# First turns of the experts: a routing cast by ScalarE, the shared down product split, y's last store on ScalarE's queue, another order of VectorE's work

## The reference, cut to what matters

```python
scores = sigmoid(tok @ router_w)
_, top_e = top_k(masked(scores + router_bias), 8)        # 4 of 8 groups, then 8 experts
wts = scores[top_e] / sum(scores[top_e]) * 2.5
for each block b of 128 tokens that chose expert e:
    xb = x_pad[rows[b]]
    hb = silu(xb @ w_gate[e]) * (xb @ w_up[e])
    y[rows[b]] += (hb @ w_down[e]) * wts
y = y + (silu(tok @ s_gate) * (tok @ s_up)) @ s_down
```

## Time and profile before

| | |
|---|---|
| median of three executions | 2744.7 us |
| the profiled execution | 2747.92 us, its span 2746.1 us |
| TensorE matmul busy | 2630.2 us, 96% |
| VectorE busy | 2019.8 us, 74% |
| ScalarE busy | 1367.0 us, 50% |
| granted TensorE clock, mean | 0.983 |

### The profile page before, as it was taken

How to read it: one execution, slowest core, us unless ns; L and a number is a source line. 1 busy time by engine, 2 the same in 40 slices (tenths; PEclk the granted TensorE clock), 3 DMA queues, 4 the chain that set the end, 5 groups by cost and what they waited for, 6 DMA issues and landing times. The chain is left out here.

```text
span 2746.1 us, 42114 instructions
## 1 busy us (share of the span) xinstructions
PE 2630.2 (96%) x13712; PEld 1193.1 (43%) x13715; DVE 2019.8 (74%) x5289; ACT 1367.0 (50%) x3178; POOL 603.2 (22%) x458
## 2 busy tenths in 40 slices
PE   7999999999899999999999799998999999999995
PEld 2444666545433443434434375453333334333332
DVE  4996566585588888888877555755897888888865
ACT  1113666343166666666656241332665666666651
POOL 0000000111023332332323211100232332333322
PEclk9999999999999999999999999998999999999998
DMA  9777400201399999999989732016999999999996
GB/s 374 252 266 200 183 17 17 78 36 47 147 366 362 335 331 342 359 347 357 371 302 366 223 115 91 31 46 250 339 338 345 311 377 346 352 372 299 327 343 203
DMA packets 151301, 697.56 MB, mean 254 GB/s; under 512 B 25189, under 2 KB 30565, under 8 KB 98857
## 3 DMA queue, kind: packets, MB, share of 16 engines
q1 hardware_dynamic: 104252, 556.14, 51.9%
q0 software_dynamic: 46528, 136.62, 20.1%
q10 hardware_dynamic: 304, 2.11, 0.2%
HBM read 597.50 MB, written 128.47 MB: 264 GB/s over the span
## 5 line engine op out<-in xcount | busy, mean ns | idle before, releaser
L1812 ACT ACTIVATE xT<-xt_blocks 32x256 f32<-32x256 f32 x2208 | 913.5, 414 | 38.4 <-DVE xt_blocks L1638 10.8
L1889 PE MATMUL exG<-ring,xT 128*32 128x512 f32 (+2 forms) x2352 | 684.8, 601 | 0.9 <-DMA ring<-in_exp_w_up_dram 0.6
L1653 DVE STREAM_TRANSPOSE ex_hT<-ex_h 32x64 f32<-32x64 f32 x2240 | 528.6, 236 | 33.6
L1889 PEld LDWEIGHTS exG<-ring,xT 128*32 128x32 f32 (+2 forms) x2352 | 240.3, 141 | 342.3 <-issue 338.5
L1550 POOL DMA_INDIRECT wide_t<-u_scratch,idx x144 | 152.8, 1061 | 946.2 <-DVE idx_out L1687 773.7
L1563 POOL DMA_INDIRECT y_scratch<-wide_w,idx_out x192 | 322.3, 1679 | 146.5 <-issue 80.1
L1922 PE MATMUL exD<-ring,ex_hT 128*32 128x512 f32 (+2 forms) x1176 | 351.6, 599 | 2.4 <-DVE wide_w L1679 2.4
L1889 PE MATMUL exG<-wide_w,xT 128*32 128x512 f32 (+2 forms) x1072 | 325.0, 601 | 11.1 <-issue 11.1
L1889 PE MATMUL exG<-wide_t,xT 128*32 128x512 f32 (+2 forms) x1024 | 315.3, 599 | 3.3 <-DVE xT L1632 2.1
L1824 ACT ACTIVATE ex_e<-exG 128x256 f32<-128x256 f32 x142 | 54.4, 383 | 524.7 <-PE exG L1889 524.7
L1643 DVE TENSOR_TENSOR ex_h<-ex_e,exG 128x256 f32<-128x256 f32 x142 | 86.5, 609 | 179.0 <-ACT ex_e L1824 178.6
(11 more groups left out here) (366 smaller groups left out, 3277.7 us busy)
## 6 DMA issues: line engine op xcount, KB each, us to landing
ring<-in_exp_w_gate_dram SPq DMA_DIRECT2D x64, 1024.0 KB
ring<-in_exp_w_up_dram SPq DMA_DIRECT2D x64, 1024.0 KB
ring<-in_exp_w_down_dram SPq DMA_DIRECT2D x64, 1024.0 KB, 12.1
wide_t<-in_exp_w_gate_dram SPq DMA_DIRECT2D x34, 1024.0 KB
wide_t<-in_exp_w_up_dram SPq DMA_DIRECT2D x34, 1024.0 KB
wide_t<-in_exp_w_down_dram SPq DMA_DIRECT2D x34, 1024.0 KB
wide_w<-in_exp_w_gate_dram SPq DMA_DIRECT2D x32, 1024.0 KB, 10.9
wide_w<-in_exp_w_up_dram SPq DMA_DIRECT2D x32, 1024.0 KB, 17.2
```

Of the source, the lines that this page charges most:

```text
L1653: last = dve.transpose(hT[m * UNIT:(m + 1) * UNIT, par].rearrange("p (k t) -> p k t", k=FK)[:, :, a * UNIT:(a + 1) * UNIT], hid[a * UNIT:( ...
L1812: last = act.activation(xT[m * UNIT:(m + 1) * UNIT, par, :, a * UNIT:(a + 1) * UNIT], parts[a * UNIT:(a + 1) * UNIT, m], ACT.Copy)
L1889: last = pe.matmul(psG[par][p:p + m], xT[:, par, k, p:p + m], ring[s % RING][:, 0:2, k * FF:(k + 1) * FF], start=k == 0, stop=k == KT - 1)
```

## The change

In **mix**: the first cast of the weights goes from VectorE (L1222) to ScalarE, which waits for VectorE's copy of the places first; the subtraction that uses it is moved ahead of the wait for turn 0's row numbers. TensorE does the first half of `down(7)` ahead of turn 0's row numbers and the second half behind them. y's last store is issued by ScalarE behind its own copy instead of by SyncE.

In **experts**: VectorE's first turns are written in another order, and TensorE's `index(2)`, `index(3)` are put between steps of `gate_up(0)`, `index(4)` between steps 2 and 3 of `gate_up(1)`; `turn_rows(1)` follows `gate_up(0)` directly.

```diff
@@ mix, SyncE
-                            sp.wait_ge(yo_done, t + 1)
-                            sp.dma_start(y_dram[layer]...[t * P:(t + 1) * P, 0], yo[t % 2]).then_inc(yo_out[t % 2], 16)
+                            else:
+                                sp.wait_ge(yo_done, t + 1)
+                                keep_y(sp, t)
@@ mix, VectorE
                         link(dve.tensor_copy(place[:], psM[:, :, 0:E]))
+                        dve.sem_inc(place_done, 1)
...
-                        dve.tensor_copy(moving[:, :, :, 3], psM[:, :, E:])
+                        dve.wait_ge(high_done, 1)
+                        link(tt(rest, psM[:, :, E:], moving[:, :, :, 3], ALU.subtract))
                         link0 = Links(dve, idx_own)
                         dve.wait_ge(first_mm, 1)
...
-                        link(tt(rest, psM[:, :, E:], moving[:, :, :, 3], ALU.subtract))
@@ mix, ScalarE
                         turn_h(a + 3)
+                        act.wait_ge(place_done, 1)
+                        act.activation(moving[:, :, :, 3], psM[:, :, E:], ACT.Copy).then_inc(high_done, 1)
                         store(7)
+                        act.wait_ge(yo_done, NT)
+                        keep_y(act, NT - 1)
@@ mix, TensorE
                         last.then_inc(ranked_mm, 1)
+                        down(7, (0,))
...
                         last.then_inc(first_mm, 1)
-                        down(7)
+                        down(7, (1,))
@@ experts, VectorE
                         indices(0, 0, 2)
-                        onehot(2, 0)
                         indices(1, 1, 2)
                         rows(0, 0, 2)
+                        onehot(2, 0)
+                        onehot(3, 1)
                         indices(2, 0, 2)
-
-                        onehot(3, 1)
+                        onehot(4, 0)
+
                         rows(1, 1, 2)
                         indices(3, 1, 2)
-                        onehot(4, 0)
                         turn_blocks(2, 0)
                         indices(4, 0, 2)
@@ experts, TensorE
                         turn_rows(0, 0, 16)
+                        gate_up(0, 0, range(0, 3))
                         index(2, 0)
-
-                        gate_up(0, 0)
+                        gate_up(0, 0, range(3, 6))
+                        index(3, 1)
+                        gate_up(0, 0, range(6, KT))
                         turn_rows(1, 1, 16)
-                        index(3, 1)
+                        gate_up(1, 1, range(0, 3))
                         index(4, 0)
+                        gate_up(1, 1, range(3, KT))
                         for b in range(1, T):
                             par = b % 2
-                            gate_up(b, par)
+                            if b > 1:
+                                gate_up(b, par)
```

More of the change, by code:

```diff
@@ L1051, in mix @@
                     "r_exp", "r_mask_done", "r_cnt_mm", "r_pos_mm", "r_iota"))
+                place_done, high_done = sem("r_place_done"), sem("r_high_done")
                 rank_done, key_mm, ids_done, cat_done, turn_mm, catT_done, ranked_mm = (sem(n) for n in (
@@ L1054, in mix, with keep_y @@
                 GONE = -3.0e38
+                def keep_y(eng, t):
+                    eng.dma_start(y_dram[layer].rearrange("(r j) d -> r j d", j=2)[t * P:(t + 1) * P, 0], yo[t % 2]).then_inc(yo_out[t % 2], 16)
                 with nc.Block(no_gpsimd_drain=True) as block:
@@ L1078, in _ @@
                                 load_down(sp, ex, 0)
-                            sp.wait_ge(yo_done, t + 1)
-                            sp.dma_start(y_dram[layer].rearrange("(r j) d -> r j d", j=2)[t * P:(t + 1) * P, 0], yo[t % 2]).then_inc(yo_out[t % 2], 16)
+                            else:
+                                sp.wait_ge(yo_done, t + 1)
+                                keep_y(sp, t)
                     @block.gpsimd
@@ L1342, in score, with down @@
                             last.then_inc(l_mm, 1)
-                        def down(t):
+                        def down(t, some=(0, 1)):
                             if t == 0:
                                 pe.wait_ge(wd_done, 1)
-                            pe.wait_ge(hT_done, t + 1)
-                            after(pe, yo_done, t, 1)
-                            for c in range(2):
+                            if some[0] == 0:
+                                pe.wait_ge(hT_done, t + 1)
+                                after(pe, yo_done, t, 1)
+                            for c in some:
                                 for k in range(FK):
@@ L1352, in down @@
                                                      start=k == 0, stop=k == FK - 1)
-                            last.then_inc(d_mm, 1)
+                            if some[-1] == 1:
+                                last.then_inc(d_mm, 1)
                         for t in range(NT):
@@ L1879, in turn_rows, with gate_up @@
                             last.then_inc(X_mm, 1)
[L1881 to L1887, removed]
+                        def gate_up(b, par, some=range(KT)):
+                            if some[0] == 0:
+                                for s, _, _, _, _ in turns[b]:
+                                    if first[s] == b:
+                                        pe.wait_ge(w_in[s % RING], 32 * (s // RING + 1))
+                                columns_ready(pe, b)
+                                after(pe, h_done, b, 2)
+                            for k in some:
                                 for s, _, p, m in pieces(turns[b]):
@@ L1890, in gate_up @@
                                                      start=k == 0, stop=k == KT - 1)
-                            last.then_inc(g_mm, 1)
+                            if some[-1] == KT - 1:
+                                last.then_inc(g_mm, 1)
                         def gate_up_over(b, i):
```

## The result

| | median | runs | ratio to before, 95% interval |
|---|---|---|---|
| before, beside the changed kernel | 2746.18 us | 8 | |
| changed kernel | 2755.14 us | 8 | 1.0031 [1.0020, 1.0041] |

The change makes the kernel slower: 0.0031 of 2746 us is 8.5 us (5.5 to 11.3). The forecast was +3.4 us, 2748.1 us, with a range of 2739.0 to 2752.5; 2755.14 lies above it.

What follows compares the result with a forecast made beforehand. TensorE, busy 96%, was taken as the bound, with early expert turns held by weight loads and VectorE's list. Terms -0.3 (layer 0), +2.5 (layer 1), +1.2 (clock) gave +3.4 us, 2748.1 us, range 2739.0 to 2752.5.

Steps and rivals of the forecast that it cites:

- Half of `down(7)` fits the idle: End of mix: half of down(7), 1.84 us, fits TensorE's 2.13 us idle; y is issued 1.65 us earlier in layer 0.
- w3 is no longer last: Layer 0: w3 up lands at 771.3, ahead of gate_up(2) at 772.3, so the load no longer holds it.
- forecast 2.5: Layer 1 experts: index(4) inside gate_up(1) makes index(5) start at 1922.65 instead of 1920.17, a loss of 2.5 us.
- the prediction's stall of layer 0: Layer 0 experts: TensorE ends gate_up(1) at 765.2 and waits 3.0 us for index(5), released by VectorE's onehot(5).
- the term -0.3 of the sum: Layer 0 experts: gate_up(2) starts at 772.3 against 772.60, so 0.3 us of the 1.9 gained is kept.
- The term of 0.6 us a layer: Stall ahead of index(5), both layers: a clock fall costing 1.6 us, 4 chances in 10, 1.2 us in all.
- The fall of before at 761.0: Layer 0: the existing 3.2 us low-clock stretch; gate_up(1) was forecast without it, ending at 765.2.
- The cast: Mix: moved from VectorE, where it took 1.87 us, to idle ScalarE; price taken as 0.7 us, bounded by 1.87.
- The next block: After mix, layer 0: begins near 739.4 instead of 741.15, worth 1.8 us to its first instructions.
- y's landing: y's last store lands 1.2 us earlier in both layers; bounds 0 to 1.65 us in layer 0, 0 to 3.3 in layer 1.
- The slower one: Rival, chance 0.15: index(4) behind the weights' wait bounds both layers and lowers the clock; +7.0 us, 2751.7 us.
- The faster rival: Rival, chance 0.18: gate_up(1)'s earlier start is kept in layer 0, layer 1 gains y's 3.3 us; -6.5 us, 2738.2 us.

Runs made afterwards that it cites:

- e3: Changed kernel with index(2) ahead of gate_up(0) and onehot(2) ahead of indices(1), as before the change; ratio to before 1.0017.
- e7: Kernel before with one edit alone, index(2) moved behind the first three steps of gate_up(0); ratio to before 1.0020.
- e4: Changed kernel with index(4) ahead of gate_up(1) instead of behind its third step; ratio to before 1.0032.
- e6: Changed kernel with TensorE's stall ahead of index(5) filled by unread transposes, 44 in layer 0 and 16 in layer 1; ratio to before 1.0020.
- e8: Changed kernel with index(2) ahead of gate_up(0), index(4) ahead of gate_up(1), onehot(5) ahead of hidden(0) and spread(0); ratio to before 0.9999.
- e10: e8 plus unread transposes in two TensorE waits, 14 ahead of down(0) in layer 0, 22 ahead of gate_up(1) in layer 1; ratio to before 0.9978.
- e1: Kernel before with only the mix edits, the experts' order left as it was; ratio to before 0.9998.

## Why the prediction was wrong

**Right.** The direction, up, was forecast. TensorE is busy for the same time. Half of `down(7)` fits the idle. `gate_up(1)` of layer 0 starts at 757.80, as forecast, and `index(4)` at 760.45 (forecast end 760.8). Part of that is luck: `gate_up(0)` started at 746.55 and not 745.8, and was shorter than forecast by as much. w3 is no longer last in layer 0: its down load is issued at 748.04 and lands 24.8 us later, 772.8, against 774.97. Layer 1 has the stall of 2.67 us where about 3 was forecast, behind `index(4)`; `gate_up(2)` is 1.8 us later, forecast 2.5. No clock fall there. e3's 2.77 us is the prediction's stall of layer 0, with `index(2)` out of the way.

**The step that failed.** "TensorE ends gate_up(1) ... and waits 3.0 us for index(5) ... Layer 0 gains 0.3 us of the 1.9." The wait was 6.12 us, and layer 0 lost 5.5: the term -0.3 of the sum should have been +5.5. The prediction charged `index(2)` its 0.36 us on TensorE and took VectorE's list to be free at `indices(4)`. It followed the dependents of `index(4)` and not those of `index(2)`: row numbers, a gather by GpSimd of 9 to 11 us from issue to landing, and `turn_blocks(2)`, which stands ahead of `indices(4)` in VectorE's list. Before, `index(2)`'s gather went out at 747.92 and VectorE reached `turn_blocks(2)` at 759.34; with a landing 11.1 us behind the issue it had 0.3 us of slack. The change moved its issue by 5.3 us. e7 shows that this alone brings such a delay, e4 that `index(4)`, which the prediction followed, was not last in layer 0.

**The clock.** The term of 0.6 us a layer (a fall of 1.6 us with 4 chances in 10) stood for a stall of 3 us. In layer 0 the fall came and cost 2.7 us in `down(0)`, shown by e6; in layer 1 none came. Behind a stall as long as the forecast one it cost 1.7 us in e3 and 2.9 in e7 (5.40 and 6.56 less 3.70). The fall of before at 761.0 did go, as the forecast's end of `gate_up(1)` at 765.2 had it; the wait behind took the gain.

**Sizes that were off without changing the sign.** The cast: 0.7 taken, 1.89 measured, as long as VectorE's own 1.87, just past the bound given, and VectorE waits 0.64 us for it. ScalarE's plain copy of as many elements from PSUM takes 0.60 us in the experts (timeline of the changed kernel):

```profile
745.71 0.60 ACT L1833 ACTIVATE xT<-exX 128x512 f32<-128x512 f32 x1 [3.85 <-PE exX L1892]
```

The Trainium skill, "ScalarE: Activation LUTs", "What ACT_TABLE_LOAD costs", gives 186 ns and 0.833 ns an element, an estimate of 0.61 us for 512; the copy agrees, and the cast is three times that. The cast writes bf16, and to every sixth place of its tile; no run shows which of the two, or whether something else, makes it slow.

The next block: 1.8 us earlier was forecast for its first instructions; it was 0.7 on TensorE behind the sort (10.70 against 11.43 us) in layer 0. y's landing: 1.2 us taken; 1.8 and 0.9 us in the changed kernel's profile, but from 1.0 us earlier to 0.9 us later in other kernels with the early store, and turn 0's rows landed 1.3 us later in layer 0 (13.8 us behind the sort against 12.5), which the prediction had at nothing.

**The rivals.** The slower one gave the sign and nearly the size (+7.0), by a chain that the runs show only in layer 1, and without the fall of the clock that it had there. Its layer 0 is refuted by e4. The faster rival's condition, `onehot(5)` done before 766 in layer 0, was reached in e8, and there the next item, `spread(0)`, was last: 0.9999, not -6.5 us.

## What to carry to other kernels

An instruction that is moved costs what hangs on it, so follow it through every engine until it meets the list that is being lengthened: here 0.36 us of TensorE carried row numbers, a gather of 9 to 11 us, and the head of VectorE's queue. Before a producer with such a tail is delayed, work out the slack between landing and use; it was 0.3 us. Where a wait of some 2 us ahead of heavy matmuls can't be avoided, small matmuls in it whose result nobody reads can turn an order that gains nothing into one that gains: 0.0021 here, in two pairs of kernels.

## What the runs showed of the hardware

- In layer 0 the granted clock fell to 0.5 for about 7 us around the end of an idle of 6.12 us, and as long behind one of 2.92 us (e7); behind 2.06 us (e8) it was low for 3.5 us. In layer 1 it didn't fall behind 2.67 us. With the waits filled by transposes it stayed at 1.00 in layer 0 (e6 and e10, 766.5 to 776.5 and 763 to 771).
- With the changed mix, whose store of 0.5 MB is issued 0.4 us behind the indirect gather of 0.5 MB and not 2.2, the gather lands 0.1 to 2.5 us later in layer 0 of three pairs of kernels; no run shows which part of the mix does it.
- ScalarE's cast of 128x512 from PSUM to every sixth bf16 of a tile took 1.89 us, its copy of 128x512 f32 0.60 us.
- Profiled executions of one kernel differ by several us from its median (e8's took 2740.73 us, its median is 2744.14; e1's 2750.05, its median 2745.29). One place where two executions differed is a later wait for weights, with and without a fall of the clock. So a difference of 0.3% is read from many executions and placed by landmarks, not by spans.
